# The first loads of a one-core decoder step: SyncE brings the first weight half in two transfers, ScalarE issues the other three behind its table load

## The reference, cut to what matters

```
xn   = rmsnorm(x, norm_mix_g)
proj = xn @ w_in                        # (288, 2048) @ (2048, 4096), split into eight strips of 512
ya   = silu(layernorm(conv31(a_val * sigmoid(a_gate)) + b))
yb   = (pooled(p) @ pool_w) * pool_scale
yc   = c_b * conv3(c_c * c_h)
yd   = d_u * (tril(W_s) @ layernorm(d_v) + b)
x    = x + concat(rmsnorm of each of ya, yb, yc, yd) @ w_out      # 2048 x 2048
h    = silu(rmsnorm(x) @ w_gate) * (rmsnorm(x) @ w_up)            # 2048 x 5632 each
y    = rmsnorm(x + h @ w_down)                                    # 5632 x 2048
```

## Time and profile before

| | us |
|---|---|
| three runs | 1177.07, 1177.55, 1177.72 |
| median | 1177.55 |
| the profiled execution, whole | 1176.95 |
| its span, first to last instruction | 1175.2 |
| TensorE busy | 1163.5 (99%) |
| VectorE busy | 763.1 (65%) |
| ScalarE busy | 501.6 (43%) |
| DMA, mean over the span | 168 GB/s |

### The profile page before, as it was taken

One profiled execution on the slowest core, in us unless ns is written; L12 is line 12 of the kernel. 1 busy time (PEld: TensorE's weight loads), 2 busy tenths in 40 slices (PEclk: granted clock), 3 DMA queues, 4 the chain that ended last, 5 costly groups with the idle time before them and its releaser, 6 DMA issues.

```text
span 1175.2 us, 22032 instructions
## 1 busy us (share of the span) xinstructions
PE 1163.5 (99%) x8718; PEld 1162.8 (99%) x8718; DVE 763.1 (65%) x1154; ACT 501.6 (43%) x624; POOL 18.4 (2%) x52
## 2 busy tenths in 40 slices
PE   9999999999999999999999999999999999999996
PEld 9999999999999999999999999999999999999996
DVE  6799999977875644754646456465565465645655
ACT  8544535446643334333343343333333333333345
POOL 0000010000000000000000000000000000000003
PEclk9999999999999999999999999999999999999998
DMA  9665555555555555545555555555555555555542
GB/s 331 209 189 167 160 149 164 171 170 165 158 168 172 163 164 164 167 145 184 161 162 165 169 165 161 161 160 170 167 163 143 181 164 170 164 161 161 163 153 86
DMA packets 105241, 197.08 MB, mean 168 GB/s; under 512 B 7792, under 2 KB 10992, under 8 KB 105200
## 3 DMA queue, kind: packets, MB, share of 16 engines
q1 hardware_dynamic: 102512, 194.34, 54.6%
q10 hardware_dynamic: 2688, 2.18, 0.6%
HBM read 193.00 MB, written 3.49 MB: 167 GB/s over the span
## 4 chain that ended last, share of the span: by engine, by line
PE 98%; DVE 0%; DMA 0%; issue 0%; ACT 0%; DVEq 0%
PE bank L1234 32%; PE bank L1236 32%; PE bank L1235 32%; PE bank L1269 1%; PE bank L1273 1%; PE bank L1277 1%; DMA x_sb<-in_x 0%; DVE x_sb L1181 0%; PE bank L1326 0%; PE bank L1212 0%; PE bank L1220 0%; DVEq L150 0%; DVE s_bc L1173 0%; PE bank L1306 0%; DVE norm L1167 0%
## 5 line engine op out<-in xcount | busy, mean ns | idle before, releaser
L707 DVE TENSOR_TENSOR wl<-raw,wh 128x1024 fp32r<-128x1024 f32 x358 | 436.1, 1224 | 355.7 <-ACT wh L465 355.2
L465 ACT ACTIVATE wh<-raw 128x1024 fp32r<-128x1024 f32 x358 | 378.9, 1060 | 600.7 <-PE bank L1236 597.1
L1234 PE MATMUL bank<-xh_sb,wh 128*128 128x288 f32 x1872 | 554.3, 296 | 0.0
L1235 PE MATMUL bank<-xl_sb,wh 128*128 128x288 f32 x1872 | 552.2, 295 | 0.0
L1236 PE MATMUL bank<-xh_sb,wl 128*128 128x288 f32 x1872 | 550.4, 294 | 0.0
L1236 PEld LDWEIGHTS bank<-xh_sb,wl 128*128 128x128 f32 x1872 | 352.6, 188 | 0.0
L1235 PEld LDWEIGHTS bank<-xl_sb,wh 128*128 128x128 f32 x1872 | 351.4, 188 | 0.0
L1234 PEld LDWEIGHTS bank<-xh_sb,wh 128*128 128x128 f32 x1872 | 350.8, 187 | 0.0
L1234 PE MATMUL bank<-mh_sb,wh 128*128 128x288 f32 x960 | 284.2, 296 | 0.0
L1235 PE MATMUL bank<-ml_sb,wh 128*128 128x288 f32 x960 | 283.2, 295 | 0.0
L1236 PE MATMUL bank<-mh_sb,wl 128*128 128x288 f32 x960 | 282.3, 294 | 0.0
(11 more groups left out here) (177 smaller groups left out, 350.9 us busy)
## 6 DMA issues: line engine op xcount, KB each, us to landing
raw<-in_w_gate SPq DMA_DIRECT2D x88, 512.0 KB, 3.7
raw<-in_w_up SPq DMA_DIRECT2D x88, 512.0 KB, 3.6
raw<-in_w_down SPq DMA_DIRECT2D x88, 512.0 KB, 3.9
raw<-in_w_in SPq DMA_DIRECT2D x62, 512.0 KB, 4.4
raw<-in_w_out SPq DMA_DIRECT2D x32, 512.0 KB, 4.2
x_sb<-in_x SPq DMA_DIRECT2D x7, 288.0 KB, 6.6
out_y<-x_sb SPq DMA_DIRECT2D x7, 288.0 KB, 2.3
raw<-in_w_in ACTq DMA_DIRECT2D x4, 256.0 KB, 5.3
```

Of the source, the lines that this page charges most:

```text
L465: act.activation(slot(wh, t), slot(raw, t), ACT.Copy).then_inc(hi_ready, 1)
L707: dve.tensor_tensor(slot(wl, t), slot(raw, t), slot(wh, t).bitcast(F32), ALU.subtract).then_inc(lo_ready, 1)
L1234: pe.matmul(banks[n][:, 0:T], W_H[:, k, cols], hi_, start=(first and k == 0), stop=False)
L1235: pe.matmul(banks[n][:, 0:T], W_H[:, k, cols], lo_, start=False, stop=False)
```

## The change

Two transfers come into SyncE's queue between x block 0 and x block 1: the first half of tile 0 in two quarters of 256 columns (128 KB each), each with a semaphore of its own. ScalarE's program loses that half, and its other three half tiles are issued after the table load and the one-element activation, which wait for a constant of GpSimd. Each quarter's high part now waits for its own quarter.

```
@@ SyncE
             sp.dma_start(gx_sb[:, 0:KD + T], a["x"][:, 0:KD + T]).then_inc(x0_landed, 16)
+            for cols, landed in ((slice(0, GRP // 2), leading_landed), (slice(GRP // 2, GRP), first_landed[0])):
+                sp.dma_start(slot(raw, 0)[:, cols], tile_source(0)[:, 0, cols]).then_inc(landed, 16)
             sp.dma_start(gx_sb[:, KD + T:KD + 2 * T], a["x"][:, KD + T:KD + 2 * T]).then_inc(x_landed[0], 16)
@@ ScalarE
-            for t in range(HALF_TILES):
-                load_half(act, t, 0, first_landed[t])
-                load_half(act, t, 1, raw_landed[t])
...
             def hi_first_half():
-                act.wait_ge(first_landed[0], 16)
-                for cols, made in ((slice(0, GRP // 2), leading_hi), (slice(GRP // 2, GRP), first_hi)):
+                for cols, landed, made in ((slice(0, GRP // 2), leading_landed, leading_hi),
+                                           (slice(GRP // 2, GRP), first_landed[0], first_hi)):
+                    act.wait_ge(landed, 16)
                     act.activation(slot(wh, 0)[:, cols], slot(raw, 0)[:, cols], ACT.Copy).then_inc(made, 1)
...
             act.wait_ge(const_ready, 1)
             table(ACT.Copy)
+            load_half(act, 0, 1, raw_landed[0])
+            for t in range(1, HALF_TILES):
+                load_half(act, t, 0, first_landed[t])
+                load_half(act, t, 1, raw_landed[t])
             act.wait_ge(x0_landed, 16)
             x_block(0)
             hi_first_half()
```

More of the change, by code:

```diff
@@ L275, in hybrid_step @@
         sgu_landed, mats_landed, hist_landed = (sem(n) for n in ("sgu_landed", "mats_landed", "hist_landed"))
-        leading_hi = sem("leading_hi")
+        leading_landed, leading_hi = sem("leading_landed"), sem("leading_hi")
         first_landed = [sem(f"first_landed{t}") for t in range(HALF_TILES)]
```

## The result

The changed kernel takes 1178.67 us (median of 16 runs, 1178.22 to 1181.27), the kernel before 1177.14 (16 runs, 1176.70 to 1179.09). The ratio is 1.0015, with a 95% interval of 1.0008 to 1.0022: slower by about 1.5 us. That lies within 0.2% for the median, and in the stated range; the forecast was a loss of 0.5 us. The profiled execution took 1178.22 us, its span is 1176.5 (before: 1175.2), so it carries 1.3 us of the loss; it is the lowest of the 16. One execution of e5, the profiled one (1616.33 us, granted clock 0.65), and one of e1 (6489.9 us) fell out of all patterns; no reading rests on them, and e11 repeats e5.

A forecast was written before the change was run, and what follows sets the result against it. TensorE, busy 99% of the span, was taken as the bound. Times to landing gave +0.65 to +0.80 us, bytes -0.75 to 0; +0.5 was taken, on the median of 1177.55: 1178.05 us, range 1176.8 to 1179.2.

The forecast's parts named there:

- The likeliest case: Whole kernel: later by 0 to 1.1 us, 1177.55 to 1178.65 us; chance 0.54.
- the rival of late issues: ScalarE's queue: table load holds the first issue until 3.6 us; +1.6 us, 1179.2 us; chance 0.12.
- The cap and where to look: Ahead of TensorE's first product: nearly all that can be won lies there, at most about 0.75 us.
- The start: TensorE's first product: first quarter lands at 4.97 after 3.7 us, product starts at 5.58, same as before.
- gain rival: Kernel start: SyncE's queue is alone until ScalarE's first data flows; -0.2 to -0.75 us, say 1177.1; chance 0.27.
- The second quarter: First half tile: issued at 1.74, landing after 4.2 us, stops TensorE for 0.7 us; second half tile +0.65 us.
- x block 1: SyncE's load moved from 1.27 to 2.21: lands at 6.41 to 6.7, nothing on top of the 0.65 us.
- the reading by times to landing: x blocks 2 and 3: the row's 5.3 us lands them at 7.97, TensorE +0.80 us; whole sum +0.65 to +0.80.
- ScalarE's issues: ScalarE's first half-tile issue: at 1.1 us, or 2.3 if it waits for table load and small activation; no added loss.
- By bytes nothing changes: x blocks 2 and 3: same transfers ahead in both queues together, landing 7.04, no delay; whole sum between -0.75 and 0.
- The clock: Rival at TensorE's start: first product beyond 7.2 us lets the clock fall; in the middle +3 us, 1180.6; chance 0.04.

The follow-up runs named there:

- e5: The kernel before, with two 8 KB transfers into a spare buffer issued by SyncE between x block 0 and x block 1: 1178.81 us, ratio 1.0015.
- e1: The kernel before, with only ScalarE's four half tiles issued behind its table load and one-element activation: 1177.33 us, ratio 1.0002.
- e11: e5 run again unchanged, for a profile at TensorE's full clock: 1178.84 us, ratio 1.0013.
- e8: The changed kernel measured again, unchanged: 1179.97 us, ratio 1.0022.
- e9: The kernel before, with the first half tile split into two quarters as ScalarE's first and second issue: 1178.25 us, ratio 1.0009.
- e4: The changed kernel, with ScalarE's three half tiles issued only when x block 0 has landed: 1181.31 us, ratio 1.0030.
- e3: The changed kernel, with the second quarter as ScalarE's first issue, not SyncE's third: 1178.32 us, ratio 1.0010.
- e7: The changed kernel, with four more warm-up matmuls between TensorE's second and third product: 1178.57 us, ratio 1.0010.
- e10: Like e5, but each of the two small transfers has 16 rows of 64 bytes, not 128: 1178.57 us, ratio 1.0010.
- e6: The changed kernel, with the second quarter and x block 1 moved from SyncE's queue to the head of ScalarE's: 1180.33 us, ratio 1.0022.

## Why the prediction was right, and where it was not

Right in direction and in range; the loss was 1.5 us and not 0.5. The likeliest case allowed a loss of up to 1.1 (1178.65 us), and the measured one, 1.5 (1178.67 us), lies beyond it. The range reaches farther only for the rival of late issues (+1.6 us), whose mechanism did not occur. So the direction and the kind of loss were foreseen, and that the size stayed inside the range is in part luck.

- **The cap and where to look**: right. Everything happened before 10.1 us, and the rest of the trace only shifted. One reading was loose: x block 0 is called the last to arrive, but by the earlier trace rows the first half tile landed later (4.71 for 4.51). The start hung on x block 0 because ScalarE takes it first.
- **The start** (forecast 5.58, no change): it came at 5.33. x block 0 needed 2.9 us instead of 3.7 with ScalarE's queue starting 0.24 us later, and the first quarter 3.5, taken as 3.7. The gain rival had this part right and missed what follows.
- **The second quarter** is the step that was mis-sized: a stop of 0.7 us was forecast, from a landing after 4.2 us. It needed 4.84 (5.0 in e8), and TensorE waited 1.24, from the third product's due time. The 4.2 came from a transfer issued 0.47 us earlier, with other neighbours in both queues. No single row would have been a safe source: the row with this very moment of issue, which the prediction set aside, gives 5.3 for the x pair, but the same pair at the same moment took 4.2 in e9, and the quarter itself took 2.7 in e4. In these runs the time to landing changed with what both queues moved meanwhile, and the sum has no term for that.
- **x block 1**: the same error, hidden. It was forecast at 6.41 to 6.7 and landed at 7.1. With the stop taken away (e3) it sets the loss, so undoing the quarter's delay alone brings back only some 0.3 us of the 1.5. The x pair landed at 7.9, as the reading by times to landing had it (7.97).
- **ScalarE's issues** at 1.1 or 2.3: they went out at 1.05, and the late-issue rival is dead (e1: +0.2 us, within noise). Its own sum was also off: from 7.23 to 8.95 are 1.72 us and not 1.6. The Trainium skill's rule of a drain behind a table load (ScalarE: Activation LUTs, section "What ACT_TABLE_LOAD costs") did not come into play: its load of 1.28 us is in the trace, the activation behind it starts at 2.10, directly at its end, and the DMAs ahead of its end.
- **By bytes nothing changes**: wrong. Its sum was -0.75 to 0, and the result is a loss. It took the two queues as one in which only the total counts; e9 and e11 show that a change in one queue moves the landings in the other at nearly the same bytes. The rule that DMAs from both engines run on the same 16 DMA engines and interleave (the Trainium skill, DMA: Bandwidth & Descriptors, "Issuing engines are not separate DMA queues") agrees with that and with e4, where the second quarter was in time once ScalarE's queue was held; it gives no landing time for a single load.
- **The clock**: forecast as a rival with a chance of 0.04 that decides at a first product beyond 7.2. The first product came at 5.33, so that condition was not met. A stop of 1.2 us inside the first half tile seems to have been enough in a part of the runs, if e7 and the clocks of e8's runs are read so. It would add up to 1.4 us to the median and explain most of the changed kernel's spread. This is argued and not shown.

What stays open: why x block 1 in e10 and e11 lands 1.9 us later for an issue 0.93 later. That ScalarE's queue took up what SyncE's left is seen; why x block 1's own packets did not come up before about 5 us is not explained. e4 shows that such an issue lands after 2.6 us when ScalarE's queue is idle. That moving ScalarE's half tiles behind the table load let x block 0 land 0.8 us sooner (in the changed kernel and e1) fits this too, since they then started 0.24 us later and x block 0 had that time alone, but no run varies only that time.

## What to carry to other kernels

At the start of a kernel, look at both queues together. Each issue on a sequencer takes 0.47 us, and here one issue more ahead of loads that are waited for cost about 1.1 us beside a busy second queue, and two cost 1.4 even when they carried only 1 KB each. With the second queue idle the same later issue did not delay the load (e4). A time to landing read off a row holds only for that row's neighbours in both queues, so give a moved transfer a range and not one number. Splitting a load gave its first part an earlier landing here and made loads behind it later, so look at which of those has the least slack (here 0.14 us). And a stop early on may cost twice, by its length and by TensorE's clock; constants multiplied into a spare bank during the stop took the slowest executions away here (e7), and a loss of 1.3 us stayed.

## What the runs showed of the hardware that was not expected

- A load of 1 KB (16 rows of 64 bytes), issued at 1.27 us, landed after 3.4 us (e10), no sooner than one of 8 KB (3.5, e11) or the 128 KB of the first quarter (3.5).
- With ScalarE's queue idle, SyncE's first four loads of 128 to 152 KB, issued from 0.81 to 2.21, landed after 2.3 to 2.7 us each (e4). Beside a running ScalarE queue, in the profiles at full clock, x block 0 took 2.3 to 3.8, and x block 1 took 3.4 to 4.2 when issued at 1.27, 4.8 to 5.6 at 1.74, 4.9 to 5.6 at 2.21, and 6.2 when it stood in ScalarE's own queue at 1.50 (e6).
- In 3.5:5 SyncE's and ScalarE's queues moved nearly the same number of packets in four profiles: 205 and 187 before, 192 and 182 in the changed kernel, 193 and 193 in e9, 288 and 286 in e11 (193 and 152 in e7). So the queue with the smaller packets moved fewer bytes.
- ScalarE's sequencer issues DMAs while its table load runs (1.05 in 0.81 to 2.09).
- TensorE's first products ran at half pace in some executions (four in 1.30 us), at full pace in others (0.77), while the clock column reads 1.00 in both.
